# Attention steps in four parts, dense blocks in quarters, and a new order of groups and rows in a three-block transformer kernel

## The reference

```python
h = rms_norm(x, g_pre)
qa, ka, va, ga, qs, ks, vs, gs, qf, kf, vf, gf, ff = jnp.split(h @ w_in, split_at, axis=-1)
# diff: 4 heads with two score maps each, softmax of both, w = p0 - lam * p1, rms norm of the output
ya = merge(diff_attention(qa, ka, va, lam, lambda_init, subln)) * jax.nn.silu(ga)
# sb: 8 heads, a = sigmoid(z) * product of (1 - sigmoid(z)) over the later keys
yb = merge(stick_breaking_attention(qs, ks, vs)) * jax.nn.silu(gs)
# fox: 8 heads, softmax of causal scores with a learned decay
yc = merge(forgetting_attention(qf, kf, vf, cum_log_f)) * jax.nn.silu(gf)
x = x + rms_norm(jnp.concatenate([ya, yb, yc], axis=-1) @ w_out, g_post)
```

## Time and profile before

| | before |
|---|---|
| median of 3 runs | 2072.43 us (2072.26 to 2073.07) |
| the profiled execution | 2071.82 us, its span 2069.9 us |
| TensorE busy | 1942.2 us, 94% |
| ACT, DVE, POOL busy | 888.1, 764.2, 660.3 us |
| mean granted clock of TensorE | 0.968 |

### The profile page before, as it was taken

How to read it: one execution, slowest core, us unless ns; L and a number is a source line. 1 busy time by engine, 2 the same in 40 slices (tenths; PEclk the granted TensorE clock), 3 DMA queues, 4 the chain that set the end, 5 groups by cost and what they waited for, 6 DMA issues and landing times.

```text
span 2069.9 us, 25679 instructions
## 1 busy us (share of the span) xinstructions
PE 1942.2 (94%) x9552; PEld 1598.2 (77%) x9552; DVE 764.2 (37%) x1393; ACT 888.1 (43%) x1743; POOL 660.3 (32%) x278
## 2 busy tenths in 40 slices
PE   8998998998899899799889989999999999999998
PEld 6876877877777778687777768888778878888886
DVE  3444555334443455534441682100252431111102
ACT  4555464344455555444443462323353343332222
POOL 2421321321233223132123343444302424444442
PEclk9999999998899999899979999999999999999999
DMA  4211211211322121121143122222201232232322
GB/s 148 91 64 49 64 60 42 84 59 55 119 81 75 49 72 62 41 82 52 41 147 97 61 92 82 92 92 92 86 7 42 101 122 92 92 102 92 102 92 92
DMA packets 44572, 163.80 MB, mean 79 GB/s; under 512 B 6192, under 2 KB 6448, under 8 KB 43824
## 3 DMA queue, kind: packets, MB, share of 16 engines
q1 hardware_dynamic: 42640, 148.65, 22.2%
q10 hardware_dynamic: 1824, 13.63, 1.7%
HBM read 155.97 MB, written 6.29 MB: 78 GB/s over the span
## 4 chain that ended last, share of the span: by engine, by line
PE 79%; DVE 11%; ACT 7%; issue 3%; DMA 0%; POOL 0%; DVEq 0%; ACTq 0%; POOLq 0%; SPq 0%
PE bank L582 11%; PE bank L583 11%; PE bank L584 11%; PE bank L585 10%; PE bank L586 10%; PE bank L587 10%; PE bank L695 3%; PE bank L713 2%; PE bank L673 1%; PE bank L719 1%; ACT probs L946 1%; PE bank L674 1%; PE bank L671 1%; PE bank L635 1%; PE bank L715 1%
## 5 line engine op out<-in xcount | busy, mean ns | idle before, releaser
L565 POOL TENSOR_TENSOR w_hl<-w_raw,w_hl 128x1024 fp32r<-128x1024 f32 x274 | 660.1, 2414 | 1385.4 <-ACT w_hl L796 1384.8
L796 ACT ACTIVATE w_hl<-w_raw 128x1024 fp32r<-128x1024 f32 x274 | 287.6, 1059 | 352.1 <-DMA w_raw<-wstream 351.6
L582 PE MATMUL bank<-act_hl,w_hl 128*128 128x512 f32 x1056 | 431.9, 409 | 4.3 <-DVE act_hl L1139 2.1
L583 PE MATMUL bank<-act_hl,w_hl 128*128 128x512 f32 x1056 | 416.8, 395 | 0.0
L584 PE MATMUL bank<-act_hl,w_hl 128*128 128x512 f32 x1056 | 416.7, 395 | 0.0
L585 PE MATMUL bank<-w_hl,act_hl 128*128 128x512 f32 x672 | 264.7, 394 | 3.4 <-POOL w_hl L565 2.3
L587 PE MATMUL bank<-w_hl,act_hl 128*128 128x512 f32 x672 | 262.2, 390 | 0.0
L586 PE MATMUL bank<-w_hl,act_hl 128*128 128x512 f32 x672 | 262.0, 390 | 0.0
L582 PEld LDWEIGHTS bank<-act_hl,w_hl 128*128 128x128 f32 x1056 | 202.7, 192 | 48.7 <-issue 5.2
L584 PEld LDWEIGHTS bank<-act_hl,w_hl 128*128 128x128 f32 x1056 | 201.3, 191 | 43.9
L583 PEld LDWEIGHTS bank<-act_hl,w_hl 128*128 128x128 f32 x1056 | 202.5, 192 | 41.0 <-issue 2.2
(11 more groups left out here) (216 smaller groups left out, 2911.1 us busy)
## 6 DMA issues: line engine op xcount, KB each, us to landing
w_raw<-wstream SPq DMA_DIRECT2D x274, 512.0 KB, 3.5
x_spill<-x_res ACTq DMA_DIRECT2D x2, 2048.0 KB, 6.9
x_res<-x_spill ACTq DMA_DIRECT2D x2, 2048.0 KB, 8.1
x_res<-x SPq DMA_DIRECT2D x4, 512.0 KB, 5.2
g_post<-post_gains ACTq DMA_DIRECT2D x4, 512.0 KB, 3.4
x_res<-x ACTq DMA_DIRECT2D x1, 2048.0 KB, 7.7
out<-x_res SPq DMA_DIRECT2D x4, 512.0 KB, 2.6
probs<-w_gates ACTq DMA_DIRECT2D x1, 1024.0 KB, 9.7
```

Of the source, the lines that this page charges most:

```text
L565: nc.gpsimd.tensor_tensor(w_hl[:, slot, 1].rearrange("p c n -> p (c n)"), w_raw[:, slot, :], w_hl[:, slot, 0].rearrange("p c n -> p (c n)" ...
L582: pe.matmul(out_ap, wh, ah, start=start, stop=False)
L583: pe.matmul(out_ap, wh, al, start=False, stop=False)
L796: nc.scalar.activation(w_hl[:, b % RING, 0].rearrange("p c n -> p (c n)"), w_raw[:, b % RING, :], ACT.Copy).then_inc(s_high_done, 1)
```

## The change

It changes the list and the place of some pieces of a step, no arithmetic except the order of rows.

- A step of every attention has four parts (`ATT_PARTS`): PE does scores in part 0, turn 0 in part 1, values in part 2, the other turns and the heads in part 3. ACT's `turned(n-1, 0)` moves behind `soften(n)` into part 1 and `row_rms` to part 2. On DVE `turned(n-1, 0)` goes to part 1, `outputs` and the `inverses` of diff to part 2; in sb `stick` of map 0 stands in part 0 and that of map 1 in part 1, behind `turned(n-1, 0)`.
- `weave` cuts blocks into quarters of one tile.
- Groups: in diff g0, v1 and both qk groups of sb are spread over all 76 parts. In sb the output groups of diff go over 20 parts, g1 over the next 20, the first qk group of fox and v2 over the last 36. In fox the output groups of sb and the second qk group over 31 parts, g2 over 21, nothing over 12, and the first block of its own output over the last 12; the rest of the output follows behind the attention.
- The rows of a head pair run from four tiles down to one (`row_tile`), and the head turns of diff, sb and fox are at steps 7, 11, 15, 18; 10, 12, 15, 18; 13, 14, 16, 18.

```diff
-HEADS_AT = {"diff": (10, 13, 16, 18), "sb": (11, 13, 16, 18), "fox": (12, 14, 16, 18), "dil": (8, 13, 17, 18)}
+HEADS_AT = {"diff": (7, 11, 15, 18), "sb": (10, 12, 15, 18), "fox": (13, 14, 16, 18), "dil": (8, 13, 17, 18)}
+ATT_PARTS = 4
...
-            rest = [half for st in dense_steps
-                    for half in ([st[:4] + ((0, 1),), st[:4] + ((2, 3),)] if st[0] == "block" else [st])]
+            rest = [tile for st in dense_steps
+                    for tile in ([st[:4] + ((j,),) for j in st[4]] if st[0] == "block" else [st])]
...
-        return [("att", l, kind, n, part) for n in range(ATT_STEPS) for part in range(2)]
+        return [("att", l, kind, n, part) for n in range(ATT_STEPS) for part in range(ATT_PARTS)]
...
-        for ki, kind in enumerate(KINDS):
-            more = ki + 1 < len(KINDS)
-            done = 2 * HEADS_AT[kind][0]
-            if ki == 0:
-                parts = [(project("g", l, 0) + project("v", l, 1), done)]
-            else:
-                parts = [(output(l, ki - 1) + project("qk", l, ki, 1), 15), (project("g", l, ki), done)]
-            parts.append((project("qk", l, ki + 1, 0) if more else [], 2 * ATT_STEPS))
-            steps += weave(parts, attention(l, kind))
-            if ki == 1:
-                steps += project("v", l, 2)
+        end = ATT_PARTS * ATT_STEPS
+        first_of = {kind: ATT_PARTS * HEADS_AT[kind][0] for kind in KINDS}
+        parts = [(project("g", l, 0) + project("v", l, 1) + project("qk", l, 1, 0) + project("qk", l, 1, 1), end)]
+        steps += weave(parts, attention(l, "diff"))
+        parts = [(output(l, 0), first_of["sb"] // 2), (project("g", l, 1), first_of["sb"]),
+                 (project("qk", l, 2, 0) + project("v", l, 2), end)]
+        steps += weave(parts, attention(l, "sb"))
+        parts = [(output(l, 1) + project("qk", l, 2, 1), 8 * ATT_PARTS - 1), (project("g", l, 2), first_of["fox"])]
+        early, *late = output(l, 2)
+        parts += [([], ATT_PARTS * (HEADS_AT["fox"][1] + 2)), ([early], end)]
+        steps += weave(parts, attention(l, "fox"))
         steps.append(("xback", l))
-        steps += tile_by_tile(output(l, len(KINDS) - 1))
+        steps += tile_by_tile(late)
...
+    def row_tile(kind, n):
+
+        return n % 4 if kind == "dil" else 3 - n % 4
...
                     if part == 0:
                         if n == 0:
                             ready(pe, l, kind)
-                        if n == 2:
-                            values_ready(pe, l, kind)
                         if n == 8 and kind != "dil":
                             ready(pe, l, kind, 1)
                         if n < 16:
                             scores(l, kind, n)
+                    elif part == 1:
                         if 0 <= n - 1 < 16:
                             turn(l, kind, n - 1, 0)
+                    elif part == 2:
+                        if n == 2:
+                            values_ready(pe, l, kind)
                         if 0 <= n - 2 < 16:
                             values(l, kind, n - 2)
...
-                        if 0 <= n - 1 < 16:
+                        if kind == "dil" and 0 <= n - 1 < 16:
                             turned(l, kind, n - 1, 0)
                         if n < 16:
                             soften(l, kind, n)
                         if kind == "dil" and 0 <= n - 1 < 16:
                             turned(l, kind, n - 1, 2)
+                    elif part == 1:
+                        if kind != "dil" and 0 <= n - 1 < 16:
+                            turned(l, kind, n - 1, 0)
+                    elif part == 2:
                         if kind == "diff" and 0 <= n - 2 < 16:
                             row_rms(l, n - 2)
...
                         if n < 16 and kind != "sb":
                             maxima(l, kind, n)
+                        if n < 16 and kind == "sb":
+                            stick(l, kind, n, 0)
+                    elif part == 1:
                         if kind in ("sb", "fox") and 0 <= n - 1 < 16:
                             turned(l, kind, n - 1, 0)
+                        if n < 16 and kind == "sb":
+                            stick(l, kind, n, 1)
+                    elif part == 2:
                         if 0 <= n - 2 < 16:
                             outputs(l, kind, n - 2)
-                        if n < 16 and kind == "sb":
-                            for a in range(2):
-                                stick(l, kind, n, a)
                         if n < 16 and kind == "diff":
                             inverses(l, kind, n)
```

More of the change, by code:

```diff
@@ L214, in plan @@
                 for a in value_maps(kind):
-                    if (a > 0) == part:
+                    if (3 if a > 0 else 1) == part:
                         take(("T", l, kind, turn, a), (BT, 0, 1)[a] if kind == "dil" else BT)
@@ L231, in plan @@
                     mark("soft", (l, kind, n, 1))
-            if 0 <= value < 16 and part == 0:
+            if 0 <= value < 16 and part == 2:
                 for a in value_maps(kind):
@@ L238, in plan @@
                     mark("rms", (l, kind, value))
-            if n in HEADS_AT[kind] and part == 1:
+            if n in HEADS_AT[kind] and part == 3:
                 p = HEADS_AT[kind].index(n)
@@ L481, in values_before @@
                 return n
-            if st[0] == "att" and 0 <= st[3] - 2 < 16 and st[4] == 0:
+            if st[0] == "att" and 0 <= st[3] - 2 < 16 and st[4] == 2:
                 n += len(value_maps(st[2]))
@@ L662, in scores @@
             def scores(l, kind, n):
-                p, i = n // 4, n % 4
+                p, i = n // 4, row_tile(kind, n)
                 for a in unit_maps(kind):
@@ L687, in turn @@
             def turn(l, kind, n, a):
-                _, nb = geometry(kind, a, n % 4)
+                _, nb = geometry(kind, a, row_tile(kind, n))
                 if earlier(("T", l, kind, n, a))[1] > 0:
@@ L1311, in inverses @@
                 if kind == "diff":
-                    _, nb = geometry(kind, 0, n % 4)
+                    _, nb = geometry(kind, 0, row_tile(kind, n))
                     r0, r1 = probs[:, p_slot(kind, n, 0), 0:nb * P], bank_of(("S", l, kind, n, 1))[:, 0:nb * P]
```

## The result

The changed kernel takes 2102.47 us, the median of four runs (2099.68 to 2106.84), against 2072.4 before: a ratio of 1.014, with a 95% interval from 1.0124 to 1.0156. It is 30 us slower. The profiled run took 2099.68 us, the lowest of the four, with a span of 2097.8; its trace is 27.9 us longer than that of before.

A forecast was written before the change was run, and what follows sets the result against it. PE bounds the kernel, its attentions losing 53 us per layer; the change makes that 23.6 (diff) + 17.1 (sb) + 18.3 (fox) + 1.9 (dense runs) = 60.9, so +16 in all: 2088 us, range 2052 to 2108.

The forecast's parts named there:

- The sign: Whole kernel: the change makes it slower, chance 0.61 with the main forecast and two slower rivals together.
- the likeliest case: Whole kernel: the main forecast, 8 us more per layer and 16 in all, 2088 us, chance 0.49.
- The walk of the stalls: PE's waits in a layer's attentions, step by step: 18.8 us in diff, 14.9 in sb, 15.4 in fox.
- Clock: Time lost at PE's lower clock per layer: 4.8 us in diff, 2.2 in sb, 2.9 in fox; 13.5 before.
- the cover: End of fox: the early output block covers 64 to 73; block k=1 then waits 2.2 us for y_low.
- fox about as before: Fox attention: loses 18.3 us per layer, 15.4 in stalls and 2.9 by the clock, about as before.
- Dense runs: PE, some 93 more dense runs per layer at 0.02 us each: 1.9 us per layer, bounds 0 and 8.4.
- Rival C: PE: dense runs cost the full 0.09 us each, 6.5 us more per layer, 2101 us; chance 0.09.
- The split of before: Kernel before, one layer's PE loss: 16 + 3 us in diff, 12.0 + 5 in sb, about 18 in fox.
- A: Diff and sb: ACT and DVE have run ahead, so the drains hide and the kernel is faster, 2058 us; chance 0.27.
- B: Whole kernel: gains and losses cancel within 4 us, 2072 us; chance 0.12.
- D: All attentions: shorter runs keep the clock at 0.93 over 413 us, 29 us per layer, 2127 us; chance 0.03.

The follow-up runs named there:

- experiment 9: Blocks woven in quarters instead of halves, against the kernel before with `inverses` ahead of `outputs` on DVE (2056.5 us): 2092.1 us, ratio 1.0093.
- experiment 1: The changed kernel with `inverses` of diff one part earlier on DVE, ahead of `outputs`: 2069.9 us, ratio 0.9978 to the kernel before.
- kernel 6: The changed kernel with `inverses` of diff ahead of `outputs` on DVE and rows from one tile up to four: 2052.22 us, ratio 0.9894.
- experiment 7: Against kernel 6, fox's first output block moved back behind the attention: 2069.16 us, ratio 0.9979 to the kernel before.

## Why the prediction was right, and where it was off

The sign, the likeliest case and the range were right: slower, 2102.5 within 2052 to 2108. The size was 30 us and not 16. By the prediction's own steps, per layer:

**The walk of the stalls held.** Single stalls of layer 0, predicted and measured: scores(3) 1.0 and 1.23; the bank behind the gate drain 1.6 and 1.97; scores(5) 3.05 and 2.62; the first head turn 1.65 and 1.91; behind the v1 drain 3.4 and 3.55; scores(11), (13), (14) 1.1, 0.6, 1.1 and 1.23, 0.97, 1.34; the bank behind qk10 1.7 and 1.60; scores(15) 3.7 and 2.45; the start of sb 6.3 and 6.07 (5.06 + 1.01); the bank behind qk20 2.2 and 2.36, and the turn behind it 1.9 and 2.02; two drains in fox 0.9 and 0.88, 1.8 and 1.81; y_hl in front of k=1 2.2 and 2.42. One was missing from the walk: the bank of g1 behind the drain of the second output group of diff, 1.70, seen as L1209 above. It is the mechanism of experiment 9. In sum the walk has 18.8 + 14.9 + 15.4 = 49.1 us, and the stalls measured are 18.9 + 15.7 + 13.2 = 47.8 (fox with the output). That the sum is so close is in part luck: in fox the walk had 10.5 us of waits for BT, of which 7.1 came, and the missed 1.70 us stand against that.

**Clock: the term that was mis-sized.** I had 4.8 + 2.2 + 2.9 = 9.9 us for the time at the lower clock, and 13.5 for the kernel before, so that the change would win 3.6 us a layer. Measured, what is left beside the stalls went from 23.6 (61.1 - 37.5) to 27.0 us (74.8 - 47.8), 3.4 us more. This one sign is 7 us a layer and 14 in all, the whole of the miss. By kind I had 4.8, 2.2 and 2.9 us for diff, sb and fox, and 8.0, 4.4 and 14.6 are left beside the stalls, so fox is the worst. In diff I had charged the lower clock only behind the three longest stalls, 1.6 us each. The trace shows what was left out in fox. Two stretches at its end in the kernel after:

```profile
496.10:506.30 10.20, 7.17 (x33) 6.46 (x33) 5.48 (x13) 3.36 (x9) 0.00 (x0) 0.50 0.00 0
509.70:523.40 13.70, 13.21 (x50) 11.35 (x50) 4.67 (x13) 3.60 (x10) 2.37 (x1) 0.50 0.01 2
```

Before, the long one there is that of the earlier trace rows; from its start to its end it lasts 13.65 us with 11.22 busy, and a short one of 3.41 us, all of it busy, stands in front of it. Now there are two long ones, and the second is the early output block that was to be the cover: PE is busy 13.21 of 13.70 us, at 0.50 all the way. Half of the 20.38 us of work in the two is lost, 10.2 us, against half of 14.63, 7.3, before; a third one of 3.4 us follows now behind the last head turn. No stall in front of them is longer than 2.1 us; there are several of them close together:

```profile
496.32 1.12 PE L700 MATMUL bank<-ident,probs 128*128 128x128 f32 x4 [2.06 <-DVE pt_hl L1338]
499.52 1.11 PE L700 MATMUL bank<-ident,probs 128*128 128x128 f32 x4 [1.39 <-DVE pt_hl L1338]
502.05 1.11 PE L735 MATMUL bank<-ident,y_tok 128*128 128x128 f32 x4 [1.41 <-DVE pt_hl L1338]
507.94 0.55 PE L700 MATMUL bank<-ident,probs 128*128 128x128 f32 x3 [0.31 <-DVE pt_hl L1338]
509.66 1.10 PE L735 MATMUL bank<-ident,y_tok 128*128 128x128 f32 x4 [1.17 <-DVE pt_hl L1338]
```

For the kernel after, "fox about as before" was therefore wrong: fox with its output lost 27.8 us against 22.0. That it is the closeness of the stalls that keeps the clock low is a reading: the kernel before has waits of 0.36, 1.17, 1.41 and 1.01 us close together in the same place, and no run varies their spacing alone.

**Dense runs.** The prediction took 0.02 us each, 1.9 a layer, with bounds 0 and 8.4; 0.8 was found, and the runs went from 69 to 148 a layer where it had 163. The first dense matmul behind a short one does take 0.31 to the next start here too, but the last short one in front of it takes less (0.03 instead of 0.11 for a transpose). Rival C is refuted.

**The split of before.** I had 19, 17 and 18 us for diff, sb and fox, and measured 21.0, 18.1 and 22.0 with the output. The part in stalls was about right; the error is again in the clock.

**The rivals.** For A I had asked whether ACT and DVE would have run ahead. In diff and at the start of sb they had not, as each drain's stall shows. But A lay closer than I put it: most of what the drains cost in diff is hidden once `inverses` no longer stands behind `outputs` (stalls of 5.8 us instead of 18.9, experiment 1), and with ascending rows as well the kernel comes to 2052, the low end of the range. B falls with the interval. D, a clock low everywhere, did not come: in the first 106 us of fox the clock is 0.98.

**What I had not weighed.** The prediction named the order "DVE still does outputs(n-2) before inverses(n)" as a fact of the change and walked each stall with it. It did not ask what the same order cost in the kernel before, where it was 16 us.

## What to carry to other kernels

When an engine's in-order queue has work that waits for a late producer in front of work that is ready and that frees a bank, swap them first: that one move was worth 16 us in the old plan and 32 in the new one. A finer weave shortens the time between a group's last block and the next group's first on the same bank, so the drain has to be walked again at each such place (where only the cut was made finer, four new waits of 1.3 to 3.8 us a layer came with it). And cost the lower clock for the dense work behind stalls of one to two microseconds too, not for the longest stalls alone. The early output block ran at half speed in the changed kernel; in kernel 6, with short rows first, the clock from 492 to 506 us, at the end of fox, is 1.00, and there the block was worth its place (experiment 7).

## What the runs showed of the hardware

- A stretch of nearly unbroken work can stay at the 1.2 GHz level for long after the stalls: 13.21 us busy of 13.70 at 0.50, as shown above, behind stalls of 0.31 to 2.06 us. In kernel 9 such a stretch, with some waits in it, lasts 40.9 us.
- The stretch between the output of layer 1 and the third block's attention has the same list in the ten kernels whose blocks are cut in quarters. It lasts 429.2 to 433.0 us in them, with 20.3 to 29.2 us at 0.50. A difference of 4 us between two versions can come from there alone.
- A change between short and dense matmuls costs PE next to nothing: by the undisturbed distances 0.8 us a layer for 79 more dense runs.
